# Six modulation projections placed one slot later, and the row gather of an expert placed behind a wait

## Time and profile before

| | us |
|---|---|
| median of 3 runs | 2836.63 |
| lowest and highest | 2836.04, 2837.03 |
| the profiled execution: its own time | 2836.63 |
| the profiled execution: its span in the trace | 2834.8 |

### The profile page before, as it was taken

The page is one execution under the profiler, slowest core; times in us unless marked ns, Lnnn a source line. Parts: engine busy times, 40 slices in busy tenths (PEclk is TensorE's granted clock), DMA queues, the critical chain, the costliest instruction groups (busy, mean ns, idle before and its releaser), DMA issues.

```text
span 2834.8 us, 35769 instructions
## 1 busy us (share of the span) xinstructions
PE 2571.5 (91%) x13990; PEld 1638.0 (58%) x13990; DVE 1390.1 (49%) x2366; ACT 434.9 (15%) x859; POOL 59.9 (2%) x103
## 2 busy tenths in 40 slices
PE   7999999999999999998999979999977987777785
PEld 6994667799899668973555434333333763332332
DVE  6764431677876447763777732232235443121123
ACT  0000312100100121001111012211210532111110
POOL 1000000000000000000000000000000000000000
PEclk9999999999999999998999989999998998898887
DMA  7568532355555743576112599999995016999996
GB/s 264 193 231 306 199 119 82 103 193 195 187 180 207 276 165 135 190 285 208 60 60 104 199 373 422 422 422 422 422 413 208 30 63 288 422 422 422 422 422 285
DMA packets 233484, 710.12 MB, mean 250 GB/s; under 512 B 12501, under 2 KB 134373, under 8 KB 177968
## 3 DMA queue, kind: packets, MB, share of 16 engines
q1 hardware_dynamic: 223328, 676.37, 61.9%
q0 software_dynamic: 9488, 31.11, 3.1%
q10 hardware_dynamic: 576, 1.35, 0.2%
HBM read 707.64 MB, written 1.15 MB: 250 GB/s over the span
## 4 chain that ended last, share of the span: by engine, by line
PE 49%; issue 28%; DMA 16%; DVE 4%; ACT 1%; SPq 1%; POOL 0%; ACTq 0%; DVEq 0%; POOLq 0%
PE work L812 35%; PE acc L812 13%; DMA ring<-in_moe_up 11%; DMA ring<-in_moe_down 2%; PE work L828 1%; DMA ring<-in_ffn_w_in 1%; DMA ring<-in_ada_w 1%; SPq L682 1%; DMA prow<-mod_rows 0%; ACT cols_x L1540 0%; DVE stats L2031 0%; DMA rows_x<-in_x 0%; DVE ring_parts L1901 0%; ACT scratch L1540 0%; DVE rows_x L2010 0%
## 5 line engine op out<-in xcount | busy, mean ns | idle before, releaser
L812 PE MATMUL work<-ring,scratch 128*64 128x512 f32 (+1 forms) x3072 | 566.1, 642 | 117.0 <-DMA ring<-in_moe_up 70.5
L812 PE MATMUL work<-rows_h_parts,ring_parts 128*128 128x256 f32 x2816 | 517.5, 284 | 14.9 <-DVE cols_x_parts L1963 13.0
L812 PEld LDWEIGHTS work<-rows_h_parts,ring_parts 128*128 128x128 f32 x2816 | 445.2, 193 | 17.9 <-issue 12.8
L812 PEld LDWEIGHTS work<-ring,scratch 128*64 128x64 f32 (+1 forms) x3072 | 153.0, 126 | 508.0 <-issue 263.6
L812 PE MATMUL work<-cols_x_parts,ring_parts 128*128 128x256 f32 x1408 | 400.2, 284 | 0.0
L1901 DVE TENSOR_TENSOR ring_parts<-ring,ring_parts 128x2048 fp32r<-128x2048 f32 x132 | 302.6, 2292 | 4.5
L812 PE MATMUL work<-cols_x,ring 128*128 128x256 f32 (+1 forms) x896 | 281.9, 475 | 6.2 <-DVE ring L2265 2.9
L812 PEld LDWEIGHTS work<-cols_x_parts,ring_parts 128*128 128x128 f32 x1408 | 272.1, 193 | 1.4
L812 PEld LDWEIGHTS work<-cols_x,ring 128*128 128x128 f32 x896 | 169.8, 191 | 114.3 <-issue 101.3
L812 PE MATMUL acc<-ring_parts,rows_h_parts 128*128 128x512 f32 x704 | 218.1, 391 | 0.0
L812 PE MATMUL work<-scratch 128*128 128x256 f32 (+4 forms) x1040 | 200.4, 380 | 9.6 <-ACT scratch L1540 5.1
(11 more groups left out here) (264 smaller groups left out, 2383.4 us busy)
## 6 DMA issues: line engine op xcount, KB each, us to landing
ring<-in_moe_gate SPq DMA_DIRECT2D x128, 1024.0 KB, 25.2
ring<-in_moe_up SPq DMA_DIRECT2D x128, 1024.0 KB, 26.3
ring<-in_moe_down SPq DMA_DIRECT2D x128, 1024.0 KB, 25.4
ring<-in_ffn_w_in SPq DMA_DIRECT2D x88, 1024.0 KB, 6.9
ring<-in_ada_w SPq DMA_DIRECT2D x48, 1024.0 KB, 9.3
ring<-in_ffn_w_out SPq DMA_DIRECT2D x44, 1024.0 KB, 6.5
ring<-in_xa_wkv SPq DMA_DIRECT2D x16, 1024.0 KB, 7.3
ring<-in_da_w_qkv SPq DMA_DIRECT2D x12, 1024.0 KB, 14.3
```

The lines of the kernel that those rows point to most:

```text
L812: ins = nc.tensor.matmul(o, lhsT, rhs, start=start, stop=stop, **kw)
```

## The change

It does two things.

1. Quad 1 leaves differential attention, and every later quad takes the place of the one before it in number: quad 1 stands where 2 stood, 2 and 3 where 3 and 4 stood, 4 where 5 stood. Quad 5 gets a new place, inside `experts(0)`, between the transposes of the probabilities and the wait for DVE's codes. The loads, the tiles, ACT's copies and POOL's stores move along. On SP all 16 loads of quads 4 and 5 now stand between Hyena's output weights and the first expert's.
2. In an expert's turn PE gathers the next expert's rows after it has waited for the products of gate and up, no longer before.

```diff
@@ make_plan @@
     plan.add("da_qkv", loads=12, tiles=12)
     plan.add("da_turn", tiles=8)
-    ada(1)()
     plan.add("da_att", tiles=3 * NT * DA_H, units=NT * DA_H)
...
-    norm("mix_norm1", before=[values(1, 1), ada(2)])
+    norm("mix_norm1", before=[values(1, 1), ada(1)])
...
-    norm("ffn_norm3", before=[ada(3), ada(4)], cols=False)
+    norm("ffn_norm3", before=[ada(2), ada(3)], cols=False)
...
         if j == NT:
-            ada(5)()
+            ada(4)()
         plan.add(f"moe_norm0_t{j}", tiles=2)
-    plan_moe(plan, 0)
+    plan_moe(plan, 0, [ada(5)])
@@ plan_moe @@
-def plan_moe(plan, layer):
+def plan_moe(plan, layer, during_choice=()):
...
     plan.add(f"router{layer}", tiles=2)
+    for fill in during_choice:
+        fill()
     plan.add(f"codes{layer}", tiles=1)
@@ SyncE @@
             load_rows_out(plan["da_qkv"].loads, io["da_w_qkv"][0], 6)
-            load_ada(1)
...
-            load_ada(2)
+            load_ada(1)
             load_cross_attention(1)
             ffn(3)
+            load_ada(2)
             load_ada(3)
-            load_ada(4)
...
             load_rows_out(plan["hy_out0"].loads, io["hy_w_out"], 2)
+            load_ada(4)
             load_ada(5)
@@ TensorE, experts @@
-            def experts(layer):
+            def experts(layer, during_choice=()):
...
                         mm(o[32 * s:32 * s + 32, j * P:(j + 1) * P], gate[:, NT * s + j, :], ident, True, True,
                            tile_full[t % 4] if j and s == streams - 1 else None, tile_position=(0, 32 * s))
+                for fill in during_choice:
+                    fill()
                 pe.wait_ge(codes_ready, layer + 1)
...
+                    for q in range(2):
+                        read_out(pe, t + 5 + q, more)
                     if not last:
                         if streams == 2:
                             pe.wait_ge(late_read, 4 * e + 2)
                         gather_rows(e + 1)
-                    for q in range(2):
-                        read_out(pe, t + 5 + q, more)
                     grouped(t + 7, n + 8, lambda kk: gated_v[:, 2 * (kk // 2 % 2) + kk % 2, kk // 4, :])
@@ TensorE, main order @@
-            ada(1)
             pe.wait_ge(padded, 1)
...
-            ada(2)
+            ada(1)
             cross_attention(1)
...
             ffn(3)
+            ada(2)
             ada(3)
-            ada(4)
...
-            ada(5)
+            ada(4)
             normed_to_cols("moe_norm0", rows_h, tiles=range(NT, 2 * NT))
-            experts(0)
+            experts(0, during_choice=[lambda: ada(5)])
@@ ScalarE, experts @@
                 copy_tile(t + 1, aff[0:rows, :], work[0:rows, (t + 1) % 4, 0:S])
+                if layer == 0:
+                    ada_out(5)
@@ GpSimd @@
             rows_until(4)
             store_mods(0)
-            rows_until(6)
-            store_mods(1)
...
             rows_until(before_ctx)
-            store_mods(2)
+            store_mods(1)
...
             rows_until(before_ctx + 10)
+            store_mods(2)
             store_mods(3)
+            rows_until(before_ctx + 12)
+            rows_until(before_ctx + 22)
             store_mods(4)
-            rows_until(before_ctx + 22)
+            rows_until(before_ctx + 27)
             store_mods(5)
```

More of the change, by code:

```diff
@@ L1740, in _ @@
                               work[:, t % 4, :].rearrange("p (k t) -> p k t", k=4))
-            ada_out(1)
             attention("da_att", DA_H, da_exps, lambda j: j + 1)
@@ L1780, in _ @@
             memory_values(1, 1)
-            ada_out(2)
+            ada_out(1)
             cross_attention(1)
@@ L1793, in _ @@
                 norm_root("ffn_norm3", j, j)
+            ada_out(2)
+            norm_root("mod_norm0", 0, 0)
             ada_out(3)
-            norm_root("mod_norm0", 0, 0)
-            ada_out(4)
             norm("mod_norm0", rooted=1)
@@ L1847, in _ @@
                     if i == NT:
-                        ada_out(5)
+                        ada_out(4)
                 for i in range(NT * s, NT * (s + 1)):
```

## The result

The kernel after the change is slower: a median of 2864.93 us (2862.83 to 2866.07, 4 runs) against 2836.83 us (2836.04 to 2837.18, 4 runs) for the kernel before, in turns on one chip. The ratio, over all 13 executions of the kernel after, is 1.0096, with a 95% interval of 1.0084 to 1.0109 (the two medians alone give 1.0099). That is 28 us; the prediction had 7.6 us, and a range up to 2850. The profiled execution took 2863.19 us, its span is 2861.4 us.

What follows compares the result with a forecast made beforehand. PE bounds the kernel up to layer 0's router, PE then DMA layer 0's experts, DMA layer 1's. 2836.6 - 5.4 (differential attention) + 13.0 (layer 0's experts) = 2844.2 us; range 2838 to 2850.

Steps and rivals of the forecast that it cites:

- What bounds the kernel: Whole kernel: PE up to layer 0's router, PE then DMA in layer 0's experts, DMA in layer 1's.
- Part two: Layer 0's router: quad 5 fills PE's wait for codes, but its loads make the DMA stream 12.5 us later.
- rival A: Layer 0's choice: quad 5's loads are hidden, only the attention gain is left, 2831.2 us; chance 0.10.
- B: Layer 0's experts: quad's loss partly made up, DMA stream only 6 to 9 us later, 2838.7 us; chance 0.12.
- D: Layer 0's choice: new quad wholly at half level, 14.1 us, expert 0 starts at 1664, 2847.3 us; chance 0.06.
- Part three: Layer 0's expert turns: gather behind the wait adds 1.75 us, at most 1.93, making turns 29.45 (29.63) us.
- the late start: Layer 0's expert 0 starting at 1659.9, the late end of the forecast 1657.9 to 1659.9.
- rival C: Layer 0's experts: PE bounds them all, serial gather drags DVE's or ACT's next step, 2854.4 us; chance 0.12.
- Part one: Differential attention: without its quad the scores start earlier, gain 5.4 us, bounds 4.9 to 7.0.
- Layer 1, 0 us: Layer 1's experts: PE idles in every turn, so the gather behind the wait costs 0 us.

Runs made afterwards that it cites:

- e1: The changed kernel with the gather put back ahead of the wait, quads still moved; 2849.77 us, 1.0042 of before.
- e5: e1 with quads 4 and 5 both ahead of the router, nothing in the choice; 2849.09 us, 1.0053 of before.
- e3: The changed kernel with a second, unsignalled gather of the same rows ahead of the wait; 2848.85 us, 1.0036 of before.
- e4: e1 with quad 5 and its loads moved behind layer 0's experts; 2841.62 us, 1.0016 of before.
- e2: The changed kernel with all quads put back, gather still behind the wait; 2864.89 us, 1.0091 of before.
- e8: The kernel before with unread matmuls added in the router's waits; 2842.95 us, 1.0015 of before.
- e9: The kernel before with only quad 5 moved behind layer 0's experts; 2840.40 us, 1.0006 of before.

## Why the prediction failed, by its own steps

**What bounds the kernel: right.** There are two paces in layer 0, 27.70 and 29.82 us, and the larger of PE's turn and DMA's decides. One reading of the slices was loose: those at 422 GB/s are 25 to 29 and 35 to 39, the ones beside them are only partly full; nothing was worked out from it.

**Part two, the quad in the choice: right.** Expert 0 starts at 1659.44, DMA has no gap, and the stream is 12.5 us later by the sum, 11.9 to 12.5 by e1 and 12.3 by e5. e1 leaves nothing of rival A (the loads are hidden) or B (a stream only 6 to 9 us later). D's quad wholly at half level did not occur: it took 8.4 us instead of 7.07 (its first matmuls start at 1645.91, its last end at 1654.30), a small part of it at half level. The codes' transposes came 2.6 us later than before, 0.6 us of which the router's later start had brought along.

**Part three, the gather behind the wait: this is the step that failed.** "1.75 us, at most the 1.93 us of its full length" was right for the gather's own length, 1.86 us by e3. It left out that in the old order the gather filled PE's wait for DVE, and that in the new one this wait stands empty, 2.33 us in each turn. That an empty wait can cost PE its clock was to be seen in the same trace, if behind a longer wait: in the choice PE idled 6.15 us and the gather behind it had matmuls of 1.06 us instead of 0.59, with a clock of 0.50 in the wait. The prediction used this in part two and not in part three, where it put the open wait at nothing without a reason. The measured terms are 27.70 + 1.86 + 0.24 = 29.80, and 8 x 1.55 / 15 = 0.83 on top, 30.63 us a turn. That it would be eight turns of 15 could not be read from the rows of before.

The margin to DMA's 29.82 was 0.2 to 0.4 us a turn, and the error was 1.0 to 1.2. By the prediction's own numbers PE decides even earlier, from (2101.86 + 12.5 - 12.2 - 1657.9) / 15 = 29.6 us a turn on, or 29.5 from the late start, and not from the 29.7 that rival C has; its own upper value of 29.63 is over that point. Rival C names the result, PE as the bound of all of layer 0. Its working with the measured turn gives 1659.9 + 15 x 30.63 + 12.2 = 2131.6, 29.7 us later than 2101.86, and 2836.6 - 5.4 + 29.7 = 2860.9 us. What C argued, that DVE's or ACT's next step drags, is not what happened. The forecast and C had opposite sides of one threshold, with chances of 0.60 and 0.12; a margin of 0.2 to 0.4 us, with the own bound on the other side, carried no such odds.

The rule that the prediction quotes from the Trainium skill, TensorE: Matmul & The Clock Gate, "HAM oscillation", that idle gaps put the array back to half rate, agrees in kind with the trace of after (0.52 behind a gap of 2.33 us, 1.00 over the 400 us of e3, where that gap is filled down to 0.24 us). The gaps in that section are longer than 2.33 us, so the page alone did not foretell part three; e3 against after shows that this gap is enough.

**Part one, 5.4 us in differential attention: mis-sized.** The prediction counts from the end of ACT's last key copy. From there to the first score it is 5.60 us in before and 0.78 to 0.82 us in the five kernels without the quad: 4.8 us are won, since the 0.2 us taken for the semaphore's way measured 0.8. To the first exponential it is 8.56 us in before and 5.17 to 5.54 us without the quad: 3.2 us are won. The other 1.6 us go to the half level of the scores. It came behind PE's wait of 2.16 to 2.19 us in after, e3, e4 and e5; in e1 the last four transposes ahead of a wait of 1.74 us already ran at it (1.11 us instead of 0.66). So the part is worth 3.2 us at the exponentials, for 5.4. What of it reaches the router is less sure. Start of the exponentials and of a norm ahead of the router, in the profiled executions:

| | exponentials us | norm's root us |
|---|---|---|
| quad there: before, e2, e8, e9 | 323.48, 323.13, 324.07, 324.82 | 1598.82, 1596.09, 1600.63, 1598.72 |
| quad gone: after, e1, e3, e4, e5 | 321.62, 319.28, 319.64, 319.39, 319.43 | 1599.45, 1594.04, 1597.20, 1596.09, 1594.17 |

The exponentials start 4.0 us earlier in the mean (323.9 to 319.9), and ahead of the router 2.4 us are left (1598.6 to 1596.2), but between executions of the same instructions lie up to 5 us: e2 did not touch that part and is 2.7 us ahead of before, and after is 5.4 us behind e1. A difference of 2.4 us between four and five such executions is not clear of zero. The profiled execution of after had drawn a late one, 0.6 us behind before. The medians speak for 0 to 2 us: e1 is 12.0 us and e5 10.2 us slower than before, and the 8 loads alone cost about 12.3 us; the profiled execution of e1 (2845.34 us) is the fastest of its nine. So of the 5.4 us at most a small part is shown to reach the kernel's time.

**Layer 1, 0 us: right.** 10.6 of the 15.0 us of the gather's wait there come out of waits for DMA, and the layer is as long as before.

The sum with the measured terms: layer 0 ends at +28.6 us, of which expert 0's start is +1.0 and the 15 turns are 459.4 against 429.0 us, +30.4. DMA's waits of the last turn, 2.8 us, are no longer there. Another 2 us come back ahead of layer 1's router, and +26.6 us is the difference of the spans. The forecast had +7.6 us. Of the 19 us between them 6 lie ahead of the router (+0.6 for -5.4), 15 in layer 0 (+28.0 for +13.0), and 2 come back.

## What to carry to other kernels

Work that stands in a wait has two values: its own length, and the idle time it covers. Before it is moved behind the wait, write down the gap that stays open, look in the same trace for a gap of that size, and read the clock of what comes after it. And when two engines' paces lie within 0.3 us of each other, the error of the estimate decides which one rules; give both sides their odds, and price both.

For prefetched loads the question is where the ring is full: loads taken away ahead of a full ring win nothing, loads added there cost whatever does not fit into DMA's empty time.

## What the runs showed of the hardware that was not expected

- A gap of 2.33 us with PE idle, once in 29.8 us, put the gather behind it on 1.2 GHz in 8 of 15 turns, in after and in e2 alike: gathers at 1.06 us mostly alternate with those at 0.61 us, and twice in 15 turns two slow ones follow each other. Filling the gap removed them all (e3). Why it is these turns, and not all, stays open.
- The same gather costs PE 1.85 us at 2.4 GHz and 3.45 us at 1.2 GHz.
- A program that issued 360 matmuls more was 16 us faster (e3 against after), with a busy PE of 2608.5 instead of 2579.0 us.
- Executions of identical instructions reach the last norm ahead of the router up to 5.4 us apart (after and e1), and 3.2 us apart on one and the same chip (e1 and e3).
